# Two-layer streaming encoder: the norm between the layers and at the end, taken by token halves

## The reference, cut to what matters

```python
def rmsnorm(x, g):
    xf = x.astype(jnp.float32)
    y = xf * lax.rsqrt(jnp.mean(xf * xf, axis=-1, keepdims=True) + EPS)
    return y.astype(x.dtype) * g

def mixer_output(x, gate, oa, ga, ob, gb, ma, mb, w_oa, w_ob, w_out):
    ya = (oa * jax.nn.silu(ga)) @ w_oa
    yb = (ob * jax.nn.silu(gb)) @ w_ob
    m = jax.nn.sigmoid(ma) * ya + jax.nn.sigmoid(mb) * yb
    return x + gate[:, None] * (m @ w_out)
...
    for l in range(DEPTH):
...
    y_prompt = rmsnorm(xp, g_final)
    y_sample = rmsnorm(xs, g_final)
```

## Time and profile before

| | us |
|---|---|
| median of 3 runs | 1230.98 |
| lowest and highest run | 1230.91, 1231.00 |
| profiled execution, its own time | 1228.15 |
| its span in the profile | 1226.4 |

### The profile page before, as it was taken

The page is one execution under the profiler, slowest core; times in us unless marked ns, Lnnn a source line. Parts: engine busy times, 40 slices in busy tenths (PEclk is TensorE's granted clock), DMA queues, the critical chain, the costliest instruction groups (busy, mean ns, idle before and its releaser), DMA issues.

```text
span 1226.4 us, 19820 instructions
## 1 busy us (share of the span) xinstructions
PE 1136.4 (93%) x7724; PEld 988.4 (81%) x7724; DVE 711.3 (58%) x1528; ACT 472.8 (39%) x1073; POOL 348.9 (28%) x208
## 2 busy tenths in 40 slices
PE   7699999988998999989999999998899999998995
PEld 4498896867887888879978889687788888888995
DVE  2527998654566765264665499956452225625556
ACT  4325445422433333332344554543243333433321
POOL 0235541210122312233333553302011222223331
PEclk9799999898999989999999999999899999999998
DMA  9363122201125443113433212120112123311331
GB/s 357 116 199 94 54 73 68 70 18 35 36 72 182 164 137 138 53 51 107 164 119 108 80 53 87 57 68 35 36 35 65 53 61 121 122 52 52 106 123 73
DMA packets 33489, 113.22 MB, mean 92 GB/s; under 512 B 4586, under 2 KB 5322, under 8 KB 31732
## 3 DMA queue, kind: packets, MB, share of 16 engines
q1 hardware_dynamic: 32068, 109.43, 27.2%
q10 hardware_dynamic: 1328, 2.53, 0.6%
HBM read 104.82 MB, written 7.12 MB: 91 GB/s over the span
## 4 chain that ended last, share of the span: by engine, by line
PE 83%; DVE 9%; ACT 3%; issue 2%; POOL 1%; DMA 1%; SPq 0%; POOLq 0%; DVEq 0%; ACTq 0%
PE pj L663 18%; PE pj L665 17%; PE pj L664 17%; PE po L934 5%; PE ps L878 3%; PE turned L906 3%; PE ps L869 2%; PE pj L823 2%; PE ps L881 1%; PE pj L797 1%; DVE probs L1445 1%; POOL w_lo L1596 1%; DVE negmax L1423 1%; PE po L923 1%; PE pj L808 1%
## 5 line engine op out<-in xcount | busy, mean ns | idle before, releaser
L663 PE MATMUL pj<-h_hi,w_hi 128*128 128x272 f32 x1776 | 533.1, 300 | 21.4 <-DVE h_lo L1300 8.3
L665 PE MATMUL pj<-h_lo,w_hi 128*128 128x272 f32 x1776 | 521.9, 294 | 0.0
L664 PE MATMUL pj<-h_hi,w_lo 128*128 128x272 f32 x1776 | 519.1, 292 | 0.0
L1596 POOL TENSOR_TENSOR w_lo<-ring,w_hi 128x1024 fp32r<-128x1024 f32 x112 | 271.2, 2421 | 639.0 <-ACT w_hi L1012 638.8
L663 PEld LDWEIGHTS pj<-h_hi,w_hi 128*128 128x128 f32 x1776 | 343.4, 193 | 35.2 <-issue 16.9
L664 PEld LDWEIGHTS pj<-h_hi,w_lo 128*128 128x128 f32 x1776 | 343.7, 194 | 0.2
L665 PEld LDWEIGHTS pj<-h_lo,w_hi 128*128 128x128 f32 x1776 | 342.4, 193 | 0.0
L1012 ACT ACTIVATE w_hi<-ring 128x1024 fp32r<-128x1024 f32 x112 | 119.0, 1062 | 144.9 <-PE pj L665 131.0
L1179 ACT ACTIVATE probs<-logit,negmax 128x128 f32<-128x128 f32 (+2 forms) x68 | 39.1, 575 | 210.8 <-DVE negmax L1432 193.8
L1432 DVE CUSTOM_DVE_ANT_0 logit<-ps,bias_p 128x128 f32<-128x128 f32 (+1 forms) x64 | 31.4, 491 | 150.8 <-PE ps L881 150.7
L1179 ACT ACTIVATE probs<-ps,negmax 128x128 f32<-128x128 f32 (+2 forms) x68 | 36.6, 538 | 160.5 <-DVE negmax L1423 141.6
(11 more groups left out here) (254 smaller groups left out, 1430.3 us busy)
## 6 DMA issues: line engine op xcount, KB each, us to landing
ring<-in_wts SPq DMA_DIRECT2D x150, 512.0 KB, 3.6
wide<-in_ada SPq DMA_DIRECT2D x3, 1024.0 KB, 21.2
ring<-in_wts SPq DMA_DIRECT2D x6, 384.0 KB, 3.1
wide<-in_xT SPq DMA_DIRECT2D x1, 2176.0 KB, 7.9
wide<-in_xT SPq DMA_DIRECT2D x2, 1088.0 KB, 5.4
x_between<-wide ACTq DMA_DIRECT2D x8, 272.0 KB, 2.1
wide<-x_between SPq DMA_DIRECT2D x2, 1088.0 KB, 5.7
bias_p<-in_ada SPq DMA_DIRECT2D x2, 1024.0 KB, 9.9
```

The lines of the kernel that those rows point to most:

```text
L663: pe.matmul(out, hi, h_hi[:, k, half(b)], start=(k == first), stop=False)
L664: pe.matmul(out, lo, h_hi[:, k, half(b)], start=False, stop=False)
L665: return pe.matmul(out, hi, h_lo[:, k, half(b)], start=False, stop=(k == stop))
L1596: pool.tensor_tensor(w_lo[:, slot, :], ring[:, ring_slot[splits[n]], :], w_hi[:, slot, :].bitcast(F32), ALU.subtract).then_inc(s_wlo, 1)
```

## The change

The sums of squares now leave out f = 7: VectorE adds the squares of f = 1 to 6, and TensorE sums that and the square of f = 7 in one PSUM group of two products. For half 0 both stand ahead of product (7, 1), and no longer in its middle. VectorE takes the reciprocal of half 0 after the evacuation of (6, 1), so ahead of that of (7, 1), and that of half 1 after it. 28 matmuls for 40 stand between the layers. The final scaling is made by halves: VectorE makes chunks 0 to 3 of half 0 between its last evacuation and the second reciprocal, and chunks 0 to 4 of half 1 after it. GpSimd makes chunks 4 to 7 of half 0 and 5 to 7 of half 1, each in two instructions: a multiply by g as soon as the chunk of x is ready, all seven of them first, and then one by the reciprocal root. SP stores 16 halves in place of 8 chunks, in the order: VectorE's four and GpSimd's four of half 0, VectorE's five and GpSimd's three of half 1. Four semaphores that each layer had for itself are now shared and counted with `past`; waits are otherwise the same there, and those lines are left out below.

```diff
@@ the final scaling
+        y = [(gate_a, gate_b)[k // 4][:, k % 4, :] for k in range(KD)]
+
+        def final_product(dve, k, b):
+            dve.scalar_tensor_tensor(out=y[k][:, half(b)], in0=xT[:, k, half(b)], scalar=g_fin[:, k:k + 1],
+                                     in1=rstd[0][:, half(b)], op0=ALU.mult, op1=ALU.mult).then_inc(f_y, 1)
...
-        added = {job: n + 1 for n, job in enumerate(j for j in last_order() if j[0])}
+        added = {job: n + 1 for n, job in enumerate(j for j in last_order() if 0 < j[0] < 7)}
@@ TensorE
                 def new_squares(b):
 
-                    pe.wait_ge(s_xsum, added[7, b])
-                    pe.matmul(ps[:, b, 0:HF], ones[:, :], squares[:, 2, half(b)], start=True, stop=True).then_inc(s_xst, 1)
+                    pe.wait_ge(s_xsum, added[6, b])
+                    pe.matmul(ps[:, b, 0:HF], ones[:, :], squares[:, 2, half(b)], start=True, stop=False)
+                    pe.wait_ge(s_xsq, past(s_xsq) + last_order().index((7, b)) + 1)
+                    pe.matmul(ps[:, b, 0:HF], ones[:, :], squares[:, 1, half(b)], start=False, stop=True).then_inc(s_xst, 1)
...
                     for k in range(KD):
-                        if job == ("wx", 7, 1) and k == KD // 2:
-
-                            new_squares(0)
...
                 for f, b in last_order():
+                    if (f, b) == (7, 1):
+                        new_squares(0)
                     project(("wx", f, b))
                 new_squares(1)
                 if not final:
-                    stay_busy(pe, 40)
+                    stay_busy(pe, 28)
@@ VectorE
                 def add_squares(n):
                     f, b = last_order()[n]
-                    if f:
+                    if 0 < f < 7:
                         dve.wait_ge(s_xsq, past(s_xsq) + n + 1)
                         acc = squares[:, 2, half(b)]
                         dve.tensor_tensor(acc, acc, squares[:, f % 2, half(b)], ALU.add).then_inc(s_xsum, 1)
                         dve.wait_ge(s_xsum, added[f, b])
+
+                def root(b):
+                    dve.wait_ge(s_xrt, b + 1)
+                    dve.reciprocal(rstd[0][:, half(b)], rstd[0][:, half(b)]).then_inc(s_rec, 1)
+                    dve.wait_ge(s_rec, past(s_rec) + b + 1)
...
                         add_squares(n - 1)
                     elif n == 13:
                         add_squares(12)
-                        add_squares(13)
-                add_squares(14)
-                add_squares(15)
-
-                for b in range(2):
-                    dve.wait_ge(s_xrt, b + 1)
-                    link(dve.reciprocal(rstd[0][:, half(b)], rstd[0][:, half(b)]))
+                    elif n == 14:
+                        add_squares(14)
+                        root(0)
+                if final:
+                    for k in range(4):
+                        final_product(dve, k, 0)
+                root(1)
+                if final:
+                    for k in range(5):
+                        final_product(dve, k, 1)
@@ GpSimd, at the end of a layer
+                if final:
+                    shares = [(k, 0) for k in range(4, 8)] + [(k, 1) for k in range(5, 8)]
+                    for k, b in shares:
+                        pool.wait_ge(s_xup, past(s_xup) + last_order().index((k, b)) + 1)
+                        pool.tensor_scalar(y[k][:, half(b)], xT[:, k, half(b)], g_fin[:, k:k + 1], None, ALU.mult).then_inc(f_x, 1)
+                    for n, (k, b) in enumerate(shares):
+                        pool.wait_ge(s_rec, past(s_rec) + b + 1)
+                        pool.wait_ge(f_x, n + 1)
+                        pool.tensor_tensor(y[k][:, half(b)], y[k][:, half(b)], rstd[0][:, half(b)], ALU.mult).then_inc(f_yp, 1)
@@ VectorE, then SP, at the end of the program
-                for k in range(KD):
-                    dve.scalar_tensor_tensor(out=(gate_a, gate_b)[k // 4][:, k % 4, :], in0=xT[:, k, :], scalar=g_fin[:, k:k + 1], in1=rstd[0],
-                                             op0=ALU.mult, op1=ALU.mult).then_inc(f_y, 1)
...
-                for k in range(KD):
-                    sp.wait_ge(f_y, k + 1)
-                    sp.dma_start(A["o_y"][:, k, :], (gate_a, gate_b)[k // 4][:, k % 4, :]).then_inc(f_out, 16)
+                for done, n, k, b in ([(f_y, k + 1, k, 0) for k in range(4)] + [(f_yp, k - 3, k, 0) for k in range(4, 8)]
+                                      + [(f_y, 5 + k, k, 1) for k in range(5)] + [(f_yp, k, k, 1) for k in range(5, 8)]):
+                    sp.wait_ge(done, n)
+                    sp.dma_start(A["o_y"][:, k, half(b)], y[k][:, half(b)]).then_inc(f_out, 16)
...
-                sp.wait_ge(f_out, 16 * KD)
+                sp.wait_ge(f_out, 16 * 2 * KD)
```

More of the change, by code:

```diff
@@ L482, in build @@
         s_xsq = sem("x_squared")
+        s_rec = sem("x_reciprocal_ready")
         s_xup = sem("x_updated")
         s_mth = sem("merge_gates_ready")
-        a_layer = {s_gin.num: 32, s_gad.num: 16, s_gat.num: 16, s_iq.num: 8, s_raw.num: 2, s_swp.num: 1, s_wtn.num: 1, s_vbf.num: 2, s_vtn.num: 2, s_lat.num: 10, s_lsq.num: 5, s_lst.num: 5, s_lrt.num: 2, s_kv.num: 8, s_qn.num: 8, s_qrw.num: 4, s_qsw.num: 4, s_qr.num: 4, s_hs.num: 4, s_xsq.num: 16, s_xup.num: 16, s_mth.num: 32}
+        s_hhi = sem("h_hi_ready")
+        s_hp = sem("h_lo_odd")
+        s_he = sem("h_lo_even")
+        s_xin = sem("x_scaled")
+        a_layer = {s_gin.num: 32, s_gad.num: 16, s_gat.num: 16, s_iq.num: 8, s_raw.num: 2, s_swp.num: 1, s_wtn.num: 1, s_vbf.num: 2, s_vtn.num: 2, s_lat.num: 10, s_lsq.num: 5, s_lst.num: 5, s_lrt.num: 2, s_kv.num: 8, s_qn.num: 8, s_qrw.num: 4, s_qsw.num: 4, s_qr.num: 4, s_hs.num: 4, s_xsq.num: 16, s_rec.num: 2, s_xup.num: 16, s_mth.num: 32, s_hhi.num: 8, s_hp.num: 4, s_he.num: 4, s_xin.num: 8}
         isteps = [(i, h) for i in (1, 2, 3, 4) for h in range(NH)]
@@ L548, in make_layer @@
             s_cache = sem(f"cache_loaded_l{layer}")
-            s_hhi = sem(f"h_hi_ready_l{layer}")
-            s_hp = sem(f"h_lo_odd_l{layer}")
-            s_he = sem(f"h_lo_even_l{layer}")
             s_vb = sem(f"v_ready_l{layer}")
@@ L564, in make_layer @@
             s_xrt = sem(f"x_root_taken_l{layer}")
-            s_xin = sem(f"x_scaled_l{layer}")
             s_q01 = sem(f"second_half_of_qi0_l{layer}")
@@ L626, in layer_sp @@
                     if (kind, t) == ("ga", 0):
-                        sp.wait_ge(s_xin, KD)
+                        sp.wait_ge(s_xin, past(s_xin) + KD)
                         if layer:
@@ L703, in layer_pe @@
                     if step < KD:
-                        pe.wait_ge(s_hp if step % 2 else s_he, step // 2 + 1)
+                        pe.wait_ge(s_hp if step % 2 else s_he, past(s_he) + step // 2 + 1)
                     for n, (tile, b, out) in enumerate(outs):
@@ L1023, in layer_act @@
                         first_sum(act, k // 2 + 1)
-                    act.wait_ge(s_xin, k + 1)
+                    act.wait_ge(s_xin, past(s_xin) + k + 1)
                     if k % 2:
                         if k >= 5:
-                            act.wait_ge(s_hp, (k - 3) // 2)
+                            act.wait_ge(s_hp, past(s_hp) + (k - 3) // 2)
                         dst = squares[:, k // 2 % 2, :]
@@ L1296, in h_rest @@
                 def h_rest(k):
-                    dve.wait_ge(s_hhi, k + 1)
+                    dve.wait_ge(s_hhi, past(s_hhi) + k + 1)
                     for g, cols in enumerate((slice(0, TP), slice(TP, NT))):
@@ L1312, in layer_dve @@
                     elif k >= 4:
-                        dve.wait_ge(s_he, k // 2 - 1)
+                        dve.wait_ge(s_he, past(s_he) + k // 2 - 1)
                     dve.scalar_tensor_tensor(out=scaled(k)[:, 0:TP], in0=xT[:, k, 0:TP], scalar=amp[:, k, 0:1],
@@ L1603, in layer_pool @@
                         rest()
-                    pool.wait_ge(s_hhi, k + 1)
+                    pool.wait_ge(s_hhi, past(s_hhi) + k + 1)
                     last = pool.tensor_tensor(h_lo[:, k, :], squares[:, k // 2 % 2, :], h_hi[:, k, :].bitcast(F32),
```

2 lines of the change are left out of this document (added).

## The result

| | before | after |
|---|---|---|
| median of 20 runs each | 1230.60 | 1234.52 |
| lowest and highest run | 1225.35, 1235.28 | 1229.67, 1237.54 |
| profiled execution, its own time | 1228.15 | 1236.19 |
| its span | 1226.4 | 1234.4 |

The ratio is 1.0032, 95% interval 1.0021 to 1.0042: the changed kernel is slower by 3.9 us, between 2.6 and 5.2. Both kernels spread over 8 to 10 us from run to run, and the profiled execution of after is one of the slower ones, of before one of the faster ones; so the 8.0 us between the spans is not the effect of the change, and has to be taken apart by stages. Two runs of one experiment, after_fill40, took 1300.6 and 1648.2 us at a mean granted clock of 0.83 and 0.63 of full, and are left out of its ratio.

What follows compares the result with a forecast made beforehand. TensorE, busy 93%, bounds the kernel, so only the turn between layers and the end could move: 1.30 + 1.05 = 2.35 on the 1226.35 span, with the runs' median 2.8 above the profiled execution, 1233.3 us; range 1229.5 to 1235.3.

Steps and rivals of the forecast that it cites:

- Turn: Between the layers: half 0's reciprocal starts the last evacuation 2.42 later, first scaling of layer 1 comes 1.30 later.
- Fillers: Between the layers: 28 fillers for 40 take 5.6 and end with the first piece of h; effect zero.
- End, evacuation: End of the program: the last evacuation waits for half 0's reciprocal and starts 1.39 later.
- End, taking turns: Last scalings: VectorE and GpSimd alternate, 0.98 a pair; half 0's four take 3.6, half 1's reciprocal ends 2.10 later.
- rival one: Last scalings: GpSimd works beside VectorE, end 2.35 less, 1229.9 us, within 0.2% of before; chance 0.20.
- End, output: Last stores: SP issues four in a row at 0.43 each, span closes 2.3 after the last starts; end costs 1.05.
- Sum: Whole kernel: turn 1.30 plus end 1.05 gives 2.35 on a span of 1226.35.
- Rival three: First steps of layer 1: fewer fillers and later h let TensorE's clock fall, costing 1 to 2, 1234.8 us; chance 0.18.
- Rival two: Turn and end: half 0's reciprocal is through before the last product, turn -0.7, 1227.1 us, 0.3% faster; chance 0.12.

Runs made afterwards that it cites:

- after_fill40: The changed kernel with 40 fillers again between the layers in place of 28; ratio to the kernel before 1.0028.
- after_again: The changed kernel measured once more, nothing altered; ratio to the kernel before 1.0040.
- root_after_last: The changed kernel with the reciprocal of half 0 moved back behind VectorE's evacuation of the last product; ratio to the kernel before 1.0006, median 1230.97 us.
- scale_on_vector: The changed kernel with GpSimd's share of the last scaling given back to VectorE; ratio to the kernel before 1.0030.
- before_fill28: The kernel before with 28 fillers for 40 and nothing else; ratio to the kernel before 1.0003.
- fill_the_waits: The changed kernel with 14 fillers between half 1's two sums in layer 0, 3 and 6 after layer 1's first two steps; ratio to the kernel before 1.0013.
- before_evacuation_late: The kernel before with two unread reciprocals and a copy on VectorE ahead of layer 0's last evacuation; ratio to the kernel before 1.0015.
- no_last_addition_filled: The version without VectorE's last addition of squares, plus 3 and 6 fillers after layer 1's first two steps; ratio to the kernel before 0.9971.
- pool_share_left_out: The changed kernel without GpSimd's instructions of the last scaling, its seven half chunks not computed but still stored; one run, 1229.08 us.
- no_last_addition: The changed kernel, half 0's sum and root earlier, last scaling on VectorE alone, VectorE's last addition of squares gone; ratio to the kernel before 0.9965.

## Why the prediction was right, and where a step was off

The time of 1234.52 lies in the range, 1.2 above the 1233.3 that was the likeliest. The two stages that the change touches came out as the forecast had them, +2.25 for +2.35. The rest of the measured 3.9 lies outside them.

*Turn.* The evacuation was to start 2.42 later and started 2.52 later; between ScalarE's root and the reciprocal lie 0.09, which I had at 0.03. Sum to root 1.09 (I had 1.16), first scaling +1.37 (I had +1.30; +1.59 in after_again). That the additional product on TensorE and ScalarE's split are hidden held; root_after_last gave back what the reciprocal in front had cost. Shown.

*Fillers.* 28 took 6.11, 0.22 each, since the clock was low for part of them. I had said their number is worth nothing; it moved no median in either direction.

*End, evacuation.* +1.45 for +1.39.

*End, taking turns.* The mechanism was right for one kind of GpSimd's instructions and wrong for the other, and the first term was mis-sized by it. I had 3.6 for the four scalings of half 0; they took 2.89 until the reciprocal started. The third and fourth each waited for a multiply by the reciprocal root and took 0.99 and 1.00. The first two met the multiply by g, and I had priced that like the others, at 0.62 of VectorE's time. It cost 0.24: the first scaling took 0.73 for 0.49, the second wasn't held at all, and both ran while GpSimd was at it. Rows 8 and 9, from which I had the price, show GpSimd's products and differences of two tensors; the form with one tensor operand was in no row, as I had written under rival one, and the sum didn't allow for it. So the reciprocal of half 1 ended 1.50 later than before, not 2.10. The five behind it took 3.75 for 3.65. That both engines together are no faster than one held: with rows 9 a pair costs 0.98, measured 0.92 from one scaling's start to the next, and scale_on_vector ends 0.29 earlier with no sharing. The rule that the prediction named from the Trainium skill (SBUF — State Buffer, "Who interferes with whom"), an exclusive lock for a whole instruction against any GpSimd instruction that reads SBUF, agrees with the trace beside the multiply by the root. Beside the multiply by g, which reads SBUF too, it doesn't: an addition with two operands in SBUF took its free 0.44 within that multiply's 0.96. Here the measurement decides.

*End, output.* In a row SP starts a store each 0.50 ((1.94 - 0.46) / 3, with 0.46 for one issue), not 0.43, so the last started 1.54 after VectorE's last scaling ended, for 1.30. The span closed 2.35 later, for 2.3. The end was +0.88 for +1.05.

*Sum.* 2.25 by stages, for 2.35. That the two are so close is in part luck: at the end 0.7 too much for the four scalings stood against some 0.4 too little for what follows the second reciprocal.

*The rest.* The measured 3.9 is 1.7 more than the stages give, though the lower end of its interval, 2.6, is near. Rival three named a place for it, the first steps of layer 1, and 1 to 2 us: there the two traces of the changed kernel lose 1.41 and 0.91 against the trace of before, with the clock down. The cause it gave, the fillers taken away, isn't borne out: neither after_fill40 nor before_fill28 moves the median. What the traces show in its place are waits of TensorE between the first steps, 0.71 and 1.34 in after: in all three kernels with fillers there the clock stays full, and fill_the_waits comes down to 1.6 us above before. But the kernel before gains 2.1 us by fillers as well, so its own trace, with the full clock, is no fair measure of its runs, and how much of the 1.7 the change itself brings stays open.

*Open.* The body of layer 1 takes 548.7 in one trace, 550.1 to 551.0 in some and 551.8 to 552.9 in others, with nothing changed in it but GpSimd's three multiplies at its end, and in the stretch at 865 to 895 the granted clock was 0.89 in before and 0.72 in after. The difference is the clock, by the table of stages; what sets the clock there isn't shown. All traces of the changed kernel with its order have the longer body but for fill_the_waits; but before_evacuation_late and no_last_addition_filled have it too. With one trace for each kernel I can't say whether the change moves it or chance does. That it adds to the 3.9 is argued, not shown.

Rival one fell with pool_share_left_out as a whole, and was nearly right for the multiply by g alone. Rival two was right in what it would take and wrong in that the change does it: the moved sum doesn't move the root, since table load and split sit in front of it. With the root moved too, and no shared port in the way, it came: turn -0.81 (I had -0.7) in no_last_addition.

## What to carry to other kernels

An instruction moved ahead of a wait is free only if its own input is there early; here the sum was moved and the root behind it was not, so a reciprocal of 1.86 that had been half hidden went in front of the last evacuation. Before work is given to GpSimd, look in the trace for what a VectorE operation with two SBUF operands takes beside it: if it is as long as both together, the sharing adds instructions and saves nothing. Look for each form of GpSimd's instructions by itself; here a product of two tensors held VectorE until its end, and in after a multiply by one number for each partition held it by 0.24 at most. And where the granted clock spreads a kernel over 8 us, take single stages from the traces and the whole from many runs; neither can be read for the other.

## What the runs showed of the hardware that I had not expected

Some twenty matmuls whose result nobody reads, put into waits that cost nothing in the chain, were worth 0.17% in the kernel before (0.08 to 0.26): in nine of eleven traces without them the clock fell in the first steps of layer 1, in no_last_addition with no wait of TensorE there above 1.01, and in the three with them, 3 and 6 in two waits between the steps and 14, 12 or none ahead of the last sum, it stayed full. In no_last_addition the same fillers kept the clock and gained no time. A matmul record of 272 columns is 0.43 at 1.2 GHz and 0.29 at 2.4, so the loss hides in a stage that looks busy (4.77 of 5.00 us from 650 to 655). The length of the body, 549 to 553 us, went step by step with its time at the lower clock, 17 to 27 us. SP starts one store of half a chunk each 0.50 when four stand in a row. And GpSimd's multiply with one tensor operand let a VectorE operation with two SBUF operands through, where its product of two tensors held one to its end.
